# Token projections of a decoder layer on one Trainium2 core: the indexer key computed with the last query chunk, plain chunks three steps ahead, the first weights handed over from the feed forward

## What is computed

```python
x = x + 0.5 * _swiglu(_rms_norm(x, ffn1_norm), ffn1_w_gate, ffn1_w_up, ffn1_w_down)
h = _rms_norm(x, mix_norm)
q, k, v, qi, ki, wi, hq, hf, hi, hg, ga, gr = _split_cols(h @ w_in)
q = _rope(_rms_norm(q.reshape(b, t, N_HEADS, HEAD_DIM), q_norm), pos)
k = _rope(_rms_norm(k.reshape(b, t, KV_HEADS, HEAD_DIM), k_norm), pos)
v = v.reshape(b, t, KV_HEADS, HEAD_DIM)
qi = _rope(qi.reshape(b, t, IDX_HEADS, IDX_DIM), pos)
ki = _rope(ki.reshape(b, t, 1, IDX_DIM), pos)[:, :, 0]
wi = wi * (IDX_HEADS ** -0.5)
```

## Time and profile before

| | |
|---|---|
| median of three runs | 2969.04 us (2973.59, 2963.03, 2969.04) |
| profiled execution, from first to last instruction | 2968.3 us |
| PE busy | 2844.5 us (96%) |
| DVE, ACT, POOL busy | 49%, 24%, 20% |
| first projection product of the stage to its last one | 828.1 to 1086.7 us |

### The profile page before, as it was taken

How to read it: one execution, slowest core, us unless ns; L and a number is a source line. 1 busy time by engine, 2 the same in 40 slices (tenths; PEclk the granted TensorE clock), 3 DMA queues, 4 the chain that set the end, 5 groups by cost and what they waited for, 6 DMA issues and landing times. The chain is left out here.

```text
span 2968.3 us, 50371 instructions
## 1 busy us (share of the span) xinstructions
PE 2844.5 (96%) x19355; PEld 2762.5 (93%) x19355; DVE 1458.1 (49%) x3118; ACT 699.9 (24%) x1354; POOL 598.9 (20%) x377
## 2 busy tenths in 40 slices
PE   8999999999789997999999989989999999999998
PEld 7999999999789985999977988979999999999998
DVE  6223333222667745999933567757362233333223
ACT  5111111111322324322113445530231111111111
POOL 0122211211221102112232122222211122212210
PEclk9999999999989999999999999999999999999999
DMA  4111111110123221234344234334211111111101
GB/s 131 43 43 49 57 49 42 45 54 21 59 75 105 77 76 36 71 109 132 112 130 133 51 91 148 100 99 146 79 43 43 43 42 56 57 42 42 50 27 59
DMA packets 239561, 213.07 MB, mean 72 GB/s; under 512 B 27106, under 2 KB 216834, under 8 KB 239298
## 3 DMA queue, kind: packets, MB, share of 16 engines
q1 hardware_dynamic: 229122, 180.85, 20.3%
q10 hardware_dynamic: 6336, 18.88, 1.7%
q0 software_dynamic: 3968, 11.54, 1.5%
HBM read 168.00 MB, written 43.21 MB: 71 GB/s over the span
## 5 line engine op out<-in xcount | busy, mean ns | idle before, releaser
L589 DVE TENSOR_TENSOR ff_prod<-ff_silu,ff_gu 128x384 f32<-128x384 f32 x132 | 68.7, 520 | 798.7 <-ACT ff_silu L403 798.6
L97 PE MATMUL ff_gu<-front_hhi,ff_whi 128*128 128x384 f32 (+1 forms) x1056 | 340.8, 323 | 2.6 <-DVE front_hlo L533 2.3
L97 PE MATMUL ff_gu<-rear_hhi,rear_branches 128*128 128x384 f32 (+1 forms) x1056 | 338.7, 321 | 1.2 <-DVE rear_hlo L573 1.2
L99 PE MATMUL ff_gu<-front_hhi,ff_wlo 128*128 128x384 f32 (+1 forms) x1056 | 339.5, 322 | 0.0
L98 PE MATMUL ff_gu<-front_hlo,ff_whi 128*128 128x384 f32 (+1 forms) x1056 | 339.4, 321 | 0.0
L98 PE MATMUL ff_gu<-rear_hlo,rear_branches 128*128 128x384 f32 (+1 forms) x1056 | 338.6, 321 | 0.0
L99 PE MATMUL ff_gu<-rear_hhi,rear_branches 128*128 128x384 f32 (+1 forms) x1056 | 338.6, 321 | 0.0
L304 POOL TENSOR_TENSOR ff_wlo<-ff_raw,ff_whi 128x1024 fp32r<-128x1024 f32 x62 | 149.2, 2428 | 581.9 <-ACT ff_whi L398 581.2
L304 POOL TENSOR_TENSOR rear_branches<-ff_raw,rear_branches 128x1024 fp32r<-128x1024 f32 x62 | 149.7, 2435 | 570.9 <-ACT rear_branches L398 570.9
L403 ACT ACTIVATE ff_silu<-ff_gu 128x384 f32<-128x384 f32 x132 | 61.3, 465 | 858.4 <-PE ff_gu L99 858.4
L97 PE MATMUL sel_proj<-front_hhi,proj_sel_whi 128*128 128x384 f32 (+1 forms) x672 | 215.6, 321 | 0.5 <-PEq L69 0.5
(11 more groups left out here) (389 smaller groups left out, 6676.4 us busy)
## 6 DMA issues: line engine op xcount, KB each, us to landing
ff_raw<-in_ffn_w_down SPq DMA_DIRECT2D x44, 512.0 KB, 3.6
ff_raw<-in_ffn_w_gate SPq DMA_DIRECT2D x42, 512.0 KB, 3.9
ff_raw<-in_ffn_w_up SPq DMA_DIRECT2D x42, 512.0 KB, 3.8
scratch_feat<-sel_stage ACTq DMA_DIRECT2D x32, 528.0 KB, 2.7
proj_sel_raw<-in_w_in SPq DMA_DIRECT2D x28, 512.0 KB, 3.6
tok_raw<-in_w_in SPq DMA_DIRECT2D x8, 1024.0 KB, 6.6
mix_pages<-in_cache_k SPq DMA_DIRECT2D x52, 128.0 KB, 2.6
merge_gates<-scratch_feat SPq DMA_DIRECT2D x36, 176.0 KB, 2.4
```

The source lines that it names most:

```text
L97: nc.tensor.matmul(out, w_hi, x_hi, start=first, stop=False)
L99: return nc.tensor.matmul(out, w_lo, x_hi, start=False, stop=last)
L589: nc.vector.tensor_tensor(prod[:, 0:w], act_out[:, b, 0:w], gu[:, b, 1, 0:w], ALU.mult).then_inc(prod_done, 1)
```

## The change

- The ki chunk is gone. Its 72 columns are computed with the last qi chunk, which becomes "qk" with 328 columns: there are eight chunks and 72 steps. `ki_in` and `ki_out` hold what belongs to ki; a qk step has a second copy on ACT, DVE's four operations of qi and behind them the six of ki, three transposes instead of two, and two copies to the two stage buffers. The ki part of step n waits until the transposes of step n - 2 are done.
- The steps are three plain ones first, then a normed one and a plain one in turn, with the plain columns three steps ahead (`LEAD`), up to the last three normed ones, which stand beside the first steps of qi; then qi and qk alone. `LOAD_AT` and `SPLIT_AT` are new.
- `Hand`: a buffer of 3 x 1024 columns that ff1 uses as its `raw` and `token_projections` as its first raw weight buffer (slots 0 and 1) and as `out` (slot 2). ff1's SP loads the first chunk (v) into it as soon as ff1's low parts are done, ahead of `scratch_x`. `total_sq` moves to slot 2. In the new stage ACT and DVE split this chunk in two halves, and PE waits for each half by itself. The raw buffer that stays in `tok` is the other one.
- The transposed chunks are stored by SP four steps later (`KEEP_LATER`) than before.
- `idle_products` makes 6 products instead of 12.

```diff
@@ feed_forward
-        raw = s.sb("raw", [P, RAW, UNIT])
+        raw = hand.room if hand else s.sb("raw", [P, RAW, UNIT])
...
-        total_sq = raw[:, 0, 0:CHW]
+        total_sq = raw[:, RAW - 1, 0:CHW]
...
+            if hand:
+                sp.wait_ge(w_lo_done, 6 * PAIRS - 1)
+                sp.dma_start(hand.first, hand.columns).then_inc(hand.first_in, 16)
@@ the tables
-CHUNKS = [("ki", 1536, 0), ("q", 0, 0), ("v", 768, 0), ("q", 256, 2), ("hv", 2632, 0), ("k", 512, 0), ("hv", 2888, CW),
-          ("qi", 1024, 0), ("qi", 1280, 2)]
-GROUPS = [(3, 4), (5, 6), (7,), (8,)]
-STEPS = [(0, 0), (0, 1)] + [(c, n + 2 * (c == 0)) for n in range(TT) for c in (1, 2, 0) if n + 2 * (c == 0) < TT]
-STEPS += [(c, n) for group in GROUPS for n in range(TT) for c in group]
-LOAD_AT = {0: 2, 3: 3, 18: 4, 24: 5, 29: 6, 37: 7, 47: 8}
-SPLIT_AT = {0: 2, 13: 3, 23: 4, 31: 5, 36: 6, 49: 7, 54: 8}
+CHUNKS = [("v", 768, 0), ("q", 0, 0), ("hv", 2632, 0), ("q", 256, 2), ("hv", 2888, CW), ("k", 512, 0), ("qi", 1024, 0),
+          ("qk", 1280, 2)]
+LEAD = 3
+PLAIN = [(c, n) for c in (0, 2, 4) for n in range(TT)]
+NORMED = [(c, n) for c in (1, 3, 5) for n in range(TT)]
+STEPS = PLAIN[:LEAD] + [step for j in range(3 * TT - LEAD) for step in (NORMED[j], PLAIN[j + LEAD])]
+STEPS += [step for n in range(LEAD) for step in (NORMED[3 * TT - LEAD + n], (6, n))]
+STEPS += [(6, n) for n in range(LEAD, TT)] + [(7, n) for n in range(TT)]
+LOAD_AT = {1: 2, 5: 3, 12: 4, 16: 5, 25: 6, 40: 7}
+SPLIT_AT = {0: 1, 6: 2, 10: 3, 17: 4, 22: 5, 35: 6, 57: 7}
@@ SP
+                if m >= KEEP_LATER and STEPS[m - KEEP_LATER][1] == TT - 1 and turns(m - KEEP_LATER):
+                    store_stage(m - KEEP_LATER)
...
-                if n == TT - 1 and turns(m):
-                    sp.wait_ge(kept_done, count(turns, m + 1))
...
+            store_stage(M - 1)
@@ PE
-            idle_products(nc, proj[:, 3, 0:P], ident, 12)
+            idle_products(nc, proj[:, 3, 0:P], ident, 6)
...
+                    if m == 0 and k % (KD // 2) == 0:
+                        pe.wait_ge(first_lo, 1 + k // (KD // 2))
@@ ACT
-            hi(0)
-            hi(1)
+            act.wait_ge(hand.first_in, 16)
+            for x in range(2):
+                k = slice(x * KD // 2, (x + 1) * KD // 2)
+                nc.scalar.activation(whi[:, 0, k, :], hand.first[:, k, :], ACT.Copy).then_inc(first_hi, 1)
...
+                if kind(m) == "qk":
+                    nc.scalar.activation(ki_in[:, m % 4, :], proj[:, m % 4, CW:QK], ACT.Copy)
@@ DVE
+            for x in range(2):
+                k = slice(x * KD // 2, (x + 1) * KD // 2)
+                dve.wait_ge(first_hi, x + 1)
+                nc.vector.tensor_tensor(wlo[:, 0, k, :], hand.first[:, k, :], whi[:, 0, k, :], ALU.subtract).then_inc(first_lo, 1)
...
+                elif kind(m) == "qk":
+                    a, b = rope(x, n, 4)
+                    done(nc.vector.tensor_tensor(out[:, slot, :].rearrange("p (h d) -> p h d", d=HD), a, b, ALU.add))
+                    if n >= 2:
+                        dve.wait_ge(turn_done, count(turns, m - 1))
+                        dve.wait_ge(ki_stored[n % 2], 32 * (n // 2))
```

More of the change, by code:

```diff
@@ L898, in token_projections @@
         rb = s.sb("rb", [P, CW])
-        out = s.sb("out", [P, 4, CW])
+        out = hand.out
         stage = s.sb("stage", [P, 2, 2, T])
@@ L929, in stores, with weights, kind_of @@
         def stores(m):
-            return {"k": 1, "v": 1, "hv": 1, "ki": 2}.get(kind(m), 0)
+            return int(kind(m) in ("k", "v", "hv"))
+        def weights(w, c):
+            if kind_of(c) == "qk":
+                wide = w[:, 0:2, :, :].rearrange("p s k c -> p (s k c)")[:, 0:KD * QK]
+                return wide.rearrange("p (k c) -> p k c", c=QK)
+            return w[:, c % WS, :, :]
+        def kind_of(c):
+            return CHUNKS[c][0]
         def stage_of(c):
@@ L1003, in _ @@
             for slot in range(2):
-                sp.wait_ge(stage_stored[slot], 16 * ((stage_of(NC) + 1 - slot) // 2))
+                sp.wait_ge(ki_stored[slot], 32 * ((TT + 1 - slot) // 2))
+            for slot in range(2):
+                sp.wait_ge(stage_stored[slot], 16 * 3)
         @block.gpsimd
@@ L1023, in turn @@
                 pe.wait_ge(out_done, m + 1)
-                for b in range(1 if kind(m) == "ki" else 2):
+                for b in range(2):
                     last = nc.tensor.transpose(turned[:, x % 2, b, :], out[:, m % 4, b * P:(b + 1) * P], ident[:, :])
+                if kind(m) == "qk":
+                    last = nc.tensor.transpose(turned[:, x % 2, 2, :], ki_out[:, STEPS[m][1] % 2, 0:2 * HD], ident[:, :])
                 last.then_inc(turn_done, 1)
-            idle_products(nc, proj[:, 3, 0:P], ident, 12)
+            idle_products(nc, proj[:, 3, 0:P], ident, 6)
             for m in range(M):
                 c, n = STEPS[m]
-                w = width(c)
-                if n == 0:
-                    pe.wait_ge(w_lo_done, c + 1)
+                w = QK if kind(m) == "qk" else CW
+                hi, lo = weights(whi, c), weights(wlo, c)
+                if n == 0 and c:
+                    pe.wait_ge(w_lo_done, c)
                 if m >= 4:
@@ L1080, in _ @@
                     act.wait_ge(out_done, m - 3)
-                nc.scalar.activation(taken[:, m % 4, 0:w], proj[:, m % 4, 0:w], ACT.Copy).then_inc(take_done, 1)
+                if kind(m) == "qk":
+                    nc.scalar.activation(ki_in[:, m % 4, :], proj[:, m % 4, CW:QK], ACT.Copy)
+                nc.scalar.activation(taken[:, m % 4, :], proj[:, m % 4, 0:CW], ACT.Copy).then_inc(take_done, 1)
                 if normed(m):
@@ L3310, in build @@
             hlo = front.sb("hlo", [P, KD, TP], F32R, side="right", align=512)
+            hand_over = Scope(nc, "over").__enter__()
+            hand = Hand(hand_over, a["w_in"])
             with Scope(nc, "x1") as x1:
```

115 lines of the change are left out of this document (70 added, 45 removed).

## The result

The changed kernel takes 2948.62 us, the median of five runs (2939.89 to 2950.43), against 2969.04 for the kernel before (five runs, 2961.62 to 2973.59). The ratio of after to before is 0.9918, with a 95% interval of 0.9902 to 0.9934. The forecast was 2942, with a range of 2933 to 2955. The profiled execution is the one of 2948.62 us, and its span is 2946.9.

What follows compares the result with a forecast made beforehand. TensorE, busy for 96% of the span, was taken as the bound. Terms -17.1 - 9.0 - 4.1 + 3.0 = -27.2 us took the profiled 2968.3 to 2941.1, and 0.7 to the median gave 2942; range 2933 to 2955.

Steps and rivals of the forecast that it cites:

- Products: Token stage: nine ki steps go, -24.1; wider qk steps add 6.1 and third transposes 0.9; sum -17.1 us.
- Start: Start of the token stage: 5.1 us lost instead of 14.1, with the first q step at about 836; -9.0 us.
- Waits in the pairs: Normed and plain steps in pairs: five low parts leave 7.5 us lost instead of 11.6; -4.1 us.
- The late store: In the pairs: storing transposed chunks later removes DVE's 4.4 us wait, and with it 6.4 us of PE wait and clock.
- End of the stage: Behind the token stage's last product: ki work and a third transpose make 5.9 us to the store instead of 2.9; +3.0.
- DVE was not the bound: Rival, pairs: DVE is the bound and every low-part block is paid whole, 23 us instead of 7.5; 2957, chance 0.10.
- SP was not the bound: Rival, pairs during page fetches: SP's queue is the bound, 16 pairs cost 38 us more; 2980, slower, chance 0.04.
- The start did gain: Rival, stage start: only the columns gain, PE stands for q weights as long as before; 9.0 less, 2951, chance 0.06.
- The rule beside the rows: Skill page's rule, stage start and pairs: PE goes cold in waits between matmul groups; taken for every wait, 2953.
- my second rival: Token stage: the clock falls at each of six waits of 1 to 3 us; +11 us, 2953, chance 0.09.

Runs made afterwards that it cites:

- the experiment with the first chunk: Changed kernel, but the first chunk (v) loaded at the start of the token stage, not in the first feed forward; 2958.55 us, ratio 0.9941.
- the last one of all: Changed kernel with low parts in pieces (first whole) and further apart, four ki_out buffers, ACT's first q high part ahead of its first copy; 2937.08 us.
- the pieces: Changed kernel with each low part on POOL made in four instructions of 512 elements instead of one of 2048; 2935.62 us, ratio 0.9879.

## Why the prediction was right, and where it was off

- **What bounds.** Right. PE was the bound before and after, and the other engines counted where it waits for them.
- **Products, -17.1.** Measured -16.6. The 328 columns had no row; the line between 256 and 384 gave 0.68 a step and the row is 0.76. The third transpose was +0.1 as taken.
- **Start, -9.0.** Measured -9.6. The first product came 2.6 us behind the barrier, within the forecast of 824 to 825 (which counts from a barrier at 822.0, so 824.6), and the q step 13.35 us behind it, 835.4 by that count. Two parts were off, against each other. The load took 5.3 us, not the 6.6 of the earlier trace rows, the median of eight loads that took up to 8.0 in the kernel before; and the high part had to wait for ACT's first copy, which I had left out. The forecast's 836 came out by a sum with one term too long and one missing, as the experiment with the first chunk and the last one of all showed. That is luck. The first step took 3.66 us and not 4.8: half of it had the full clock.
- **Waits in the pairs, -4.1.** Measured -3.5. I had 7.5 left, the trace has 8.1. The cause was as stated, shown by the pieces (6.1 to none) and by the low parts further apart (6.1 to 2.5). The total came out better than its parts. I had put 1.3 us on each of five low parts and 0.7 more on one. By the distances between first products, the five cost 0 (850.14), 4.2 with the low clock (862.89), 1.2, 1.6 and 1.2. What goes with it in all ten low parts of two kernels was not in my sum: whether the low part holds a copy of a plain step or an operation of a normed one. I also took 11.6 us and the 8.7 us of waits for one thing, though 0.73 of the waits lie at the end of the stage. By the count of the earlier trace rows PE's waits for DVE are 8.9 us and not below 8, as I had said they would be. No wait is over 3 us, none of DVE's in the pairs is for a store.
- **The late store.** The wait that it removed was shown by putting the store back, at 6.8 us in the new order.
- **End of the stage, +3.0.** This is the term that failed, at +4.6. From last product to the store of qiT it is 6.1 us, where 2.9 were: +3.2, as forecast. What failed is "A second store is issued behind it, 0.4, but is the smaller", by which it cost nothing. The page of the changed kernel for 1060 to 1072 us has the two (KB, us from issue to landing):

```profile
scratch_qiT<-tok_stage SPq DMA_DIRECT2D x1, 1056.0 KB, 4.1
scratch_kiT<-tok_stage SPq DMA_DIRECT2D x1, 528.0 KB, 5.0
```

  Half the bytes, issued 0.42 later, and it lands 0.42 + 5.0 - 4.1 = 1.3 us behind the other. The transfers go at some 350 to 450 GB/s in this stretch, with the two stores as with the one in the kernel before, and 528 KB at 420 GB/s are 1.3 us, by estimate; so I read it as the two sharing one rate. No run stored them in another order or apart. The barrier behind it moves by about that: the next stage begins 5.97 us behind the store of qiT instead of 4.56.
- **The rivals.** DVE was not the bound: a sum of 8.1 us and not 23, and with the blocks cut it costs nothing. Of the six waits of 1 to 3 us the clock fell behind two, the longest of those in the pairs and that of 2.45 us at the end, where only transposes follow, so a part of that rival came true, at 1.3 us. SP was not the bound (its queue costs DVE nothing in the pairs), though the experiment with the early store shows how near it was. The start did gain.
- **The rule beside the rows.** The clock stayed at 1.00 behind waits of 1.39, 1.18 and 1.05 us and fell to 0.50 behind that of 2.61. The length of the wait alone doesn't say it. With one plain step ahead, a wait of 2.62 us at the same low part left the clock at 1.00, by PE's timeline and a window of that run:

```profile
874.81 0.41 PE L1068 MATMUL tok_turned<-core_ident,over_hand 128*128 128x128 f32 x2 [2.62 <-DVE over_hand L1227]
...
874.00:878.00 4.00, 3.19 (x27) 1.00 0.13 41
```

  And the wait of 1.74 us for the q weights, with the low part in pieces, was followed by 0.54. The Trainium skill, page TensorE: Matmul & The Clock Gate, section Loop structure matters more than you think, has PE go cold at a "long DMA wait between every matmul". It doesn't say that each short wait costs, so my second rival took the page further than it goes; the rows bear out neither that nor a rule by the length of the wait.
- **The number.** The forecast for the span was 2941.1, and 2946.9 was measured: 2.1 us of the 5.8 are the stage's terms, and 3.7 the other stages, in which the recurrence alone was 9.6 longer than in the profile before. The second execution of either kernel has no such difference.

**What stays open.** Outside of the stage, the spans are equal on average: 2698.3 us in three profiles of the kernel before (one with its low parts in pieces), and 2698.4 in the ten of the changed kernel and its variants, which lie between 2684 and 2708. The medians less the stage's length are not quite: about 2698 for the former, about 2702 for the latter, with single kernels between 2694 and 2707. Whether some 4 us come back outside of the stage in most runs, or the medians of 4 to 12 runs scatter so, these runs don't tell. No experiment was aimed at it.

## What to carry over

When two engines share a path into memory, ask of each long instruction what it blocks, not only how long it takes: four short ones in place of it, or the same ones begun at other steps, took 6.1 us of waits to none and to 2.5, on an engine that was only half busy. Ask also which work it holds: a block that fell on a plain step's copy cost nothing here. A queue that waits for a late result holds up all behind it, so put the wait where the result is long there. And at the end of a stage the last transfer to land counts, with all that share its path, not the one you moved.

## What the runs showed of the hardware

- The attention took 193 to 204 us and the recurrence 201 to 217 in thirteen profiled executions, though no edit touches them, with 4 to 39 us of low clock in each. The first feed forward took 798.8 to 800.0, and the selection 380.0 to 383.0. Changes of under 5 us can't be read from whole runs here, though the stage shows them.
- A wait of 1.74 us in one kernel was followed by low clock (0.54 in 2 us), and one of 2.62 in another was not (1.00 in 4 us). Waits of 1.05 to 1.39 us in the changed kernel were not; in the kernel before, one of 1.19 behind the idle products was, 1.4 us into the products (0.50 from 830 to 832 us).
- Four GpSimd subtractions of 512 elements took 5.30 us, one of 2048 took 4.55; a blocked VectorE operation took 1.3 to 1.4 us behind each. A `COPY` with one input was held for 4.60 us too.
- A 528 KB store issued 0.42 us behind one of 1056 KB landed 1.3 us later than it; at the same place with one store alone, the 1056 KB took 4.0.
